# Gate products by one level of Strassen's algorithm, and a first layer without lead tiles

## The reference

```
h = _layer_norm(DN_ALPHA * h + u, ln2_g[i], ln2_b[i])
h = h + jax.nn.sigmoid(h @ ple_gate_w[i]) * (p[i] @ ple_w[i])
```

## Time and profile before

| | |
|---|---|
| three runs, median (lowest, highest) | 1969.9 us (1968.17, 1971.81) |
| profiled execution: its time | 1970.78 us |
| profiled execution: span, first to last instruction | 1969.0 us |
| mean granted TensorE clock | 0.998 |
| PE busy | 1945.6 us, 99% |
| DVE, POOL, ACT busy | 60%, 19%, 18% |
| chain that ended last | 90% PE, 4% issue, 2% DVE |

### The profile page before, as it was taken

The page is one execution under the profiler, slowest core; times in us unless marked ns, Lnnn a source line. Parts: engine busy times, 40 slices in busy tenths (PEclk is TensorE's granted clock), DMA queues, the critical chain, the costliest instruction groups (busy, mean ns, idle before and its releaser), DMA issues.

```text
span 1969.0 us, 33213 instructions
## 1 busy us (share of the span) xinstructions
PE 1945.6 (99%) x12520; PEld 1491.1 (76%) x12520; DVE 1181.2 (60%) x2268; ACT 351.0 (18%) x826; POOL 375.0 (19%) x485
## 2 busy tenths in 40 slices
PE   9999999999999999999999999999999999999998
PEld 7865994458769944599748869994799568769973
DVE  4343987533639875356754647666776636457674
ACT  2342000011420000300014522000200025321001
POOL 0000206310102064110130620004110303511012
PEclk9999999999999999999999999999999999999999
DMA  8422545534225454354443216444644443235443
GB/s 326 134 93 66 192 171 194 191 108 138 65 97 205 165 202 178 117 193 168 169 177 118 87 60 210 171 172 154 254 170 172 171 150 129 66 105 201 165 171 129
DMA packets 83806, 305.45 MB, mean 155 GB/s; under 512 B 9360, under 2 KB 10000, under 8 KB 83408
## 3 DMA queue, kind: packets, MB, share of 16 engines
q1 hardware_dynamic: 81360, 294.83, 42.6%
q0 software_dynamic: 2304, 8.65, 1.3%
HBM read 302.13 MB, written 1.05 MB: 154 GB/s over the span
## 4 chain that ended last, share of the span: by engine, by line
PE 90%; issue 4%; DVE 2%; ACT 1%; DVEq 0%; ACTq 0%; DMA 0%; POOL 0%; SPq 0%; POOLq 0%
PE psum L455 31%; PE psum L562 22%; PE psum L1022 13%; PE psum L2633 5%; PE psum L2033 4%; PE psum L467 3%; PE psum L337 3%; PE psum L248 2%; PE psum L326 2%; PE psum L1892 1%; PE psum L464 1%; PE psum L313 1%; PE psum L292 1%; PE psum L3019 1%; DVE x L873 0%
## 5 line engine op out<-in xcount | busy, mean ns | idle before, releaser
L455 PE MATMUL psum<-sq,space 128*128 128x128 f32 x2784 | 345.9, 275 | 1.6 <-DVE sq L659 1.6
L455 PEld LDWEIGHTS psum<-sq,space 128*128 128x128 f32 x2784 | 327.9, 192 | 2.2 <-issue 2.1
L754 POOL TENSOR_TENSOR cat<-space 128x128 f32<-128x128 f32 x76 | 57.9, 762 | 797.3 <-PE psum L562 550.6
L562 PE MATMUL psum<-space,cat 128*128 128x512 f32 x456 | 207.2, 592 | 0.0
L562 PEld LDWEIGHTS psum<-space,cat 128*128 128x128 f32 x456 | 86.4, 190 | 109.3 <-issue 109.3
L562 PE MATMUL psum<-ring,space 128*128 128x512 f32 x304 | 141.8, 592 | 0.0
L1022 PE MATMUL psum<-h,ring 128*128 128x256 f32 x544 | 124.5, 382 | 0.0
L455 PE MATMUL psum<-h,ring 128*128 128x128 f32 x928 | 122.6, 275 | 0.0
L455 PE MATMUL psum<-h,space 128*128 128x128 f32 x928 | 122.6, 275 | 0.0
L455 PE MATMUL psum<-sq,ring 128*128 128x128 f32 x928 | 120.9, 275 | 0.0
L439 DVE TENSOR_TENSOR space<-ring 128x512 f32<-128x512 f32 x76 | 59.4, 781 | 92.3 <-PE psum L562 92.3
(11 more groups left out here) (439 smaller groups left out, 3010.1 us busy)
## 6 DMA issues: line engine op xcount, KB each, us to landing
ring<-in_weights SPq DMA_DIRECT2D x551, 512.0 KB, 4.1
space<-in_rows POOLq DMA_DIRECT2D x8, 512.0 KB, 4.8
space<-in_gains POOLq DMA_DIRECT2D x6, 512.0 KB, 4.7
const<-in_consts SPq DMA_DIRECT2D x1, 1397.0 KB, 10.3
h<-in_x SPq DMA_DIRECT2D x4, 256.0 KB, 4.7
x<-in_x_tok SPq DMA_DIRECT2D x1, 1024.0 KB, 16.8
out<-x SPq DMA_DIRECT2D x2, 512.0 KB, 2.8
space<-in_params POOLq DMA_DIRECT2D x2, 509.5 KB, 4.8
```

What stands on the lines that cost most here:

```text
L455: last = pe.matmul(out, weights(i), tokens(i), start=(i == 0), stop=(i == 3), skip_group_check=True)
L562: return pe.matmul(k.psum[:, bank, :], lhs, rhs, start=(p == 0), stop=(p == fn.downs - 1), skip_group_check=True)
```

## The change

- `LEADS` becomes all zero: Ffn(2) opens with `first_jobs` and has 22 jobs in place of four leads and 18 jobs. POOL makes the weight sums of its job 0 when the layer-1 gate is summed; PE waits for three of the four summed quarters ahead of job 1.
- The gate product becomes one Strassen product over four pairs of row tiles (k, k + 4): parts 1, 2, 3, 6, 5, 7, 4, each four products of 128x512. DVE makes four token sums into `cat` and eight weight sums, POOL the other eight; part 3 waits for the token sums, part 6 for DVE's weight sums, part 7 for POOL's. DVE recombines the parts into four quarters; each goes through sigmoid, product with the embedding and sum.
- The embedding product goes column half by column half into the same banks, and ACT copies it to SBUF (`emb`), since the parts need banks 4 to 6.
- In layer 1 the first RMS norm of the second block uses half squares, so that the first half can be taken before the second is there.
- The order of the gate's units in memory goes pair by pair.

```diff
-LEADS, FIRST, TAIL, HELD = (0, 0, 4, 0, 0, 0), 4, 4, 4
+LEADS, FIRST, TAIL, HELD = (0, 0, 0, 0, 0, 0), 4, 4, 4
+PAIRS = KD // 2
+GATE_PARTS = 7
-FIRST_JOBS_AFTER = (border(0, 0, LN1), border(0, 1, LN1), border(1, 0, 1), border(1, 0, 2), border(1, 1, 1))
+FIRST_JOBS_AFTER = (border(0, 0, LN1), border(0, 1, LN1), border(0, 1, PLE), border(1, 0, 1), border(1, 0, 2), border(1, 1, 1))
...
-        pe_ffn(k, s, pe, w, Ffn(2 + 2 * l), g - 1, g, 5 if l else 4, k.h_tok, True, (k.y_half, 4 * l) if l else None)
+        pe_ffn(k, s, pe, w, Ffn(2 + 2 * l), g - 1, g, 5 if l else 4, k.h_tok, True, (k.y_half, 4 * l) if l else (k.gate_summed, 4 * LAYERS - 1))
...
+        else:
+            pool.wait_ge(k.gate_summed, 4 * LAYERS)
+            pool_first_sums(k, s, pool, Ffn(2))
...
@@ tail_tensor
+    pe.wait_ge(f.emb_copied, 4 * layer + 1)
+    for p in range(PAIRS):
+        last = part(1, p)
...
+    for p in range(PAIRS):
+        last = part(2, p)
+    last.then_inc(f.gate_parts, 1)
+    pe_normed(k, pe, ln2, 1)
+    pe.wait_ge(f.gate_tokens, layer + 1)
+    for p in range(PAIRS):
+        last = part(3, p)
+    last.then_inc(f.gate_parts, 1)
+    pe.wait_ge(f.emb_copied, 4 * layer + 3)
+    for p in range(PAIRS):
+        pe.wait_ge(f.gate_left, PAIRS * layer + p + 1)
+        last = part(6, p)
+    last.then_inc(f.gate_parts, 1)
+    for p in range(PAIRS):
+        last = part(5, p)
+    last.then_inc(f.gate_parts, 1)
+    for p in range(PAIRS):
+        pe.wait_ge(f.gate_right, PAIRS * layer + p + 1)
+        last = part(7, p)
+        if p < PAIRS - 1:
+            last.then_inc(k.freed, 2)
+    last.then_inc(f.gate_parts, 1)
+    for p in range(PAIRS):
+        if p == (3 if layer == LAYERS - 1 else 2):
+            pe_turn_h(k, pe, ple, 0, k.h_tok if layer == LAYERS - 1 else k.x_tok)
+        last = part(4, p)
...
@@ tail_scalar
+    squash(0, 0, 0)
     if layer == LAYERS - 1:
         act.wait_ge(s.params, 16)
+        act.wait_ge(f.x_half_new, 1)
+        act_half_square(k, s, act, 0, k.x_tok[:, 0, 0:512], 1.0, RMS_EPS)
+        squash(1, 0, 1)
+        act_root_table(k, act)
         act.wait_ge(s.x_new, 1)
+        act_root_of_sum(k, s, act, 0, k.x_tok[:, 0, 512:1024], 1.0).then_inc(s.x_std, 1)
+        squash(2, 1, 1)
+        act_first_turned(k, s, act, n, 0, "ffn1_pre_g")
+        squash(3, 1, 0)
+        act.wait_ge(f.x_half_new, 2)
+        act_half_square(k, s, act, 1, k.x_tok[:, 1, 512:1024], 1.0, RMS_EPS)
+        act_root_table(k, act)
         act.wait_ge(s.x_new, 2)
+        act_root_of_sum(k, s, act, 1, k.x_tok[:, 1, 0:512], 1.0).then_inc(s.x_std, 1)
+        act_first_turned(k, s, act, n, 1, "ffn1_pre_g")
         return
...
@@ tail_vector
+    dve.wait_ge(k.h_low, 2 * ln2 + 2)
+    dve.drain()
+    dve.tensor_tensor(x[:, 0, :, :], first[:, :, high], second[:, :, high], ALU.add)
+    dve.tensor_tensor(x[:, 2, :, :], first[:, :, low], first[:, :, high], ALU.subtract)
+    dve.drain()
+    dve.tensor_tensor(x[:, 1, :, :], x[:, 0, :, :], first[:, :, low], ALU.subtract)
+    dve.drain()
+    dve.tensor_tensor(x[:, 3, :, :], second[:, :, low], x[:, 1, :, :], ALU.subtract).then_inc(f.gate_tokens, 1)
+    for p in range(PAIRS):
+        b11, b12, _, _ = gate_unit_halves(k, dve, layer, p)
+        dve.tensor_tensor(f.sums[:, p, 0, :], b12, b11, ALU.subtract)
+    dve.drain()
+    for p in range(PAIRS):
+        _, _, _, b22 = gate_unit_halves(k, dve, layer, p)
+        dve.tensor_tensor(f.sums[:, p, 1, :], b22, f.sums[:, p, 0, :], ALU.subtract).then_inc(f.gate_left, 1)
...
+    dve.tensor_tensor(y(0, 0), k.copied, k.psum[:, 0, :], ALU.add).then_inc(k.gate_summed, 1)
...
+    gated(0, 0, 0)
+    added(0, 0).then_inc(f.x_half_new if last_layer else k.h_scaled, 1)
...
+    dve.tensor_tensor(y(1, 0), k.upper, k.psum[:, 2, :], ALU.subtract).then_inc(k.gate_summed, 1)
...
@@ tail_pool, behind the residual terms of LN2
+    for p in range(PAIRS):
+        _, b12, _, b22 = gate_unit_halves(k, pool, layer, p)
+        pool.tensor_tensor(f.sums[:, p, 2, :], b22, b12, ALU.subtract)
+    for p in range(PAIRS):
+        _, _, b21, _ = gate_unit_halves(k, pool, layer, p)
+        pool.wait_ge(f.gate_left, PAIRS * layer + p + 1)
+        pool.tensor_tensor(f.sums[:, p, 3, :], f.sums[:, p, 1, :], b21, ALU.subtract).then_inc(f.gate_right, 1)
```

More of the change, by code:

```diff
@@ L3014, in tail_tensor @@
     pe.wait_ge(k.parts_free, layer + 1)
[L3015 to L3018, removed]
+    rows = [pe_take(k, pe, w) for _ in range(2)]
+    for tt in range(2):
+        for b in range(2):
+            for c in range(2):
                 last = pe.matmul(k.psum[:, 4 + 2 * tt + b, :], f.embed[:, layer * 2 + c, half(tt)],
-                                 unit[:, b * 512:b * 512 + 512], start=(c == 0), stop=(c == 1), skip_group_check=True)
-                if tt + b == 0:
+                                 rows[c][:, b * 512:b * 512 + 512], start=(c == 0), stop=(c == 1),
+                                 skip_group_check=True)
+                if tt + b + c == 0:
@@ L3022, in tail_tensor @@
                     pe_hand_back(k, w, last)
-        w.owed += 1
+            last.then_inc(f.emb_ready, 1)
+    w.owed += 2
     pe_turn_h(k, pe, ln2, 1, k.h_tok)
     pe_normed(k, pe, ln2, 0)
[L3027 to L3032, removed]
+    units = [(pe_take(k, pe, w), pe_take(k, pe, w)) for _ in range(PAIRS)]
@@ new lines, in part @@
+    def part(name, p):
+        (a, c), sums, x = units[p], f.sums[:, p, :, :], f.gate_x
+        bank, lhs, rhs = {
+            1: (4, k.h[:, p, half(0)], a[:, 0:512]), 2: (0, k.h[:, PAIRS + p, half(0)], c[:, 0:512]),
+            3: (1, x[:, 3, p, :], c[:, 512:1024]), 4: (2, k.h[:, PAIRS + p, half(1)], sums[:, 3, :]),
+            5: (6, x[:, 0, p, :], sums[:, 0, :]), 6: (5, x[:, 1, p, :], sums[:, 1, :]),
+            7: (3, x[:, 2, p, :], sums[:, 2, :])}[name]
+        return pe.matmul(k.psum[:, bank, :], lhs, rhs, start=(p == 0), stop=(p == PAIRS - 1), skip_group_check=True)
@@ L3035, in tail_scalar, with embedding @@
+    last.then_inc(f.gate_parts, 1)
 def tail_scalar(k, f, s, act, w, layer):
+    def embedding(tt, b):
+        i = 2 * tt + b
+        act.wait_ge(f.emb_ready, 4 * layer + i + 1)
+        act.activation(f.emb[:, tt, b * 512:b * 512 + 512], k.psum[:, 4 + i, :], ACT.Copy).then_inc(f.emb_copied, 1)
     def norm(which, gain, bias):
@@ L3047, in norm @@
             last.then_inc(k.h_low, 1)
+            if which == LN2:
+                for b in range(2):
+                    embedding(tt, b)
     norm(LN1, "ln1_g", "ln1_b")
@@ L3145, in tail_vector @@
     norm(LN2, "ln2_g", "ln2_b")
[L3146 to L3151, removed]
-        dve.drain()
[L3153 to L3160, removed]
+    n, ln2 = border(0, layer, PLE), border(0, layer, LN2)
@@ new lines, in tail_vector @@
+    low, high, x = half(0), half(1), f.gate_x
+    first, second = k.h[:, 0:PAIRS, :], k.h[:, PAIRS:KD, :]
+    dve.wait_ge(k.h_low, 2 * ln2 + 2)
[6 more added lines that the diff above has]
+    dve.tensor_tensor(x[:, 3, :, :], second[:, :, low], x[:, 1, :, :], ALU.subtract).then_inc(f.gate_tokens, 1)
@@ new lines, in tail_vector @@
+    dve.drain()
+    dve.tensor_tensor(y(1, 1), k.upper, k.psum[:, 6, :], ALU.add).then_inc(k.gate_summed, 1)
+    if last_layer:
+        dve_rms_gained(k, s, dve, n, -1, 0, "ffn1_pre_g")
+    else:
+        turned_high(0)
+    gated(2, 1, 1)
+    dve.wait_ge(f.gate_parts, at + 7)
+    dve.tensor_tensor(y(1, 0), k.upper, k.psum[:, 2, :], ALU.subtract).then_inc(k.gate_summed, 1)
+    right = added(1, 1)
+    if last_layer:
+        right.then_inc(f.x_half_new, 1)
+    gated(3, 1, 0).then_inc(k.y_done, 1)
@@ new lines, in tail_vector, with gate_unit_halves @@
+    left = added(1, 0)
+    if last_layer:
+        left.then_inc(s.x_new, 1)
+        dve_rms_gained(k, s, dve, n, -1, 1, "ffn1_pre_g")
+    else:
+        left.then_inc(k.h_scaled, 2)
+        turned_high(1)
+def gate_unit_halves(k, eng, layer, p):
+    out = []
+    for j in range(2):
+        u = FFN_UNITS[layer] + 2 * FF1 + 2 + 2 * p + j
+        eng.wait_ge(k.filled[u % RING], 16 * (u // RING + 1))
+        out += [k.ring[:, u % RING, 0:512], k.ring[:, u % RING, 512:1024]]
+    return out
@@ L3428, in first_tail_units @@
     units = ffn_units([v["mlp_w1"][l]], v["mlp_w2"][l], LEADS[l])
-    gate, ple = list(v["ple_gate_w"][l].reshape(KD, P, UNIT)), list(v["ple_w"][l].reshape(2, P, UNIT))
-    return units + ple + gate
+    gate, ple = v["ple_gate_w"][l].reshape(KD, P, UNIT), list(v["ple_w"][l].reshape(2, P, UNIT))
+    return units + ple + [gate[p + half] for p in range(PAIRS) for half in (0, PAIRS)]
 def first_params(v):
```

68 lines of the change are left out of this document (55 added, 13 removed).

## The result

The changed kernel takes 1974.7 us (median of 20 runs, 1971.4 to 1976.4) against 1970.2 for the one before (20 runs, 1968.0 to 1973.5): ratio 1.0020, 95% interval 1.0014 to 1.0027. The forecast was 1972.7 in 1965 to 1977. The interval leaves out 1, so the change makes the kernel slower by 0.14 to 0.27%. The profiled execution has a span of 1974.4 us and a time of 1976.2.

What follows compares the result with a forecast made beforehand. TensorE, busy 1945.6 of 1969.0 us, was taken as the bound; 10.4 us of work and 0.4 of old wait removed against new waits gave +2.8 us, or 1972.7 us on the median's scale, range 1965 to 1977.

Steps and rivals of the forecast that it cites:

- Work removed, 10.4 us: TensorE work saved: 3.43 us in each of two gates and 3.57 us from replacing Ffn(2)'s lead tiles.
- The engines take turns: VectorE and GpSimd wait for each other's whole SBUF-to-SBUF instruction; turns of 0.55 us for VectorE, 0.96 or 1.12 for GpSimd's sums.
- Rival 1: The engines hardly hold each other up: no waits in the gates, -8.4 us, 1961.5; chance 0.17.
- Rival 2: GpSimd keeps VectorE out for its full 1.27 us in every sum: +5.4 us, 1975.3, slower; chance 0.20.
- Each gate 1.0 us later: In both layers' gates, 4.4 us of new TensorE waits stand against 3.43 us of work removed.
- Opening of Ffn(2), 0.95 and 3.75 us of waits: Second block's start: TensorE waits 0.95 us at the second token half's transposes and 3.75 us in job 0's blocks.
- No cost behind job 4, none from the copies, the ring or POOL's memset: Ffn(2)'s later jobs, the embedding copies, the weight units and GpSimd's wait behind the memset were to add no time.
- rival 3: Ffn(2) without leads falls behind later on VectorE's added sums: 3 to 4 us more than forecast, 1976; chance 0.08.
- The sum, +2.8 us: Whole kernel: work -10.4, old wait -0.4, gates +4.4 twice, opening +0.95 and +3.75, restarts +0.1.
- the 0.1 us allowed for restarts: Over all waits on the path: each restarts TensorE a few hundredths of a us later than counted, +0.1 in all.

Runs made afterwards that it cites:

- e3: The changed kernel with GpSimd's gate weight sums cut from 512 to 8 columns, the rest not computed; layer 0's gate takes 24.91 us.
- e4: The changed kernel with all sixteen weight sums of a gate on VectorE and none on GpSimd; ratio 0.9985 to the kernel before.
- e6: The changed kernel with twelve of sixteen gate weight sums on VectorE, GpSimd making part 4's four behind them; ratio 0.9983 to the kernel before.
- e2: The kernel before's gates kept, only the four lead tiles of Ffn(2) replaced by four more Strassen jobs; ratio 1.0018 to the kernel before.
- e7: The changed kernel with e6's gate sums and the weight sums of Ffn(2)'s job 0 on VectorE; ratio 0.9965 to the kernel before.

## Why the prediction was right, and where its numbers were off

- *Work removed, 10.4 us.* Right. Where no sum of GpSimd's is in the way (e3), layer 0's gate is 3.43 us shorter to the hundredth.
- *The engines take turns.* Right, with 1.12 us for GpSimd's turn and 0.55 for VectorE's. I forecast the token sums' ends, counted from the gate's start, at 5.06, 6.71 and 8.36 us; they came at 5.11, 6.78 and 8.45. Rival 1 (no hold, 1961.5) fell with the 2.84 us; e3, which makes its condition nearly true in the gates, shows its gates' price. Rival 2 (a full 1.27 us per turn, 1.82 in all) isn't what the trace shows: 1.67. The Trainium skill ("SBUF — State Buffer", section "SBUF: two separate sides") has an exclusive lock, taken for the whole instruction, between a VectorE instruction with two SBUF inputs and one of GpSimd's that reads SBUF. The trace agrees on the blocking (2.84 us for 0.69), and a sum with one input in PSUM isn't held (0.67 us); but the turn is shorter than the instruction's shown duration, 1.12 of 1.27 us. Two sums of the rivals are off, with no effect on the reading: rival 1's terms give -8.15 us, not -8.4, and rival 2's +5.4 leaves out the 0.5 us that the opening already costs in the forecast.
- *Each gate 1.0 us later.* Mis-sized: 1.63 and 1.70. The idle times add up to 4.05 us, less than the 4.4 forecast, but idle time is not all that a wait costs. By the pitch of 0.429 us the first instruction of part 3 was due at 404.66 + 16 x 0.429 = 411.52 and came at 413.25: 1.73 us for a wait shown as 1.56, since the record of the matmul before runs 0.16 us over its pitch. Counted so, part 3 is delayed by 1.73 us (1.6 forecast), part 6 by 1.95 (1.8) and by 0.47 + 0.81 (1.0), and 0.11 are lost behind it: 5.07 us, of which 3.43 are earned back. The shortfall, some 0.6 us a gate and 1.3 us in both, lies for the most part in VectorE's chain. Its last weight sum for part 6 was drawn 17.26 us behind the gate's start (420.3) and ended at 17.78 (422.44), 0.52 late. 0.34 of that is one term: the forecast gave GpSimd's sums of the form "space<-space,ring" a turn of 0.96 us, from the 1.09 us of the earlier trace rows, and counted 1.50 us for a pair; the last three of VectorE's sums came 1.67 apart, so the turn was 1.12. The trace of the kernel before had this price: in the first block, where the gates lie, GpSimd's sum of the same form takes 1.27 us in both layers, and 1.09 only in the second block. What makes the two differ isn't shown.

```profile
199.28 1.27 POOL L740 TENSOR_TENSOR space<-space,ring 128x512 f32<-128x512 f32 x1 [0.51 <-issue]
```

Another 0.09 is the token sums' late end, and the rest of the shortfall is small delays along the chain and PE's restarts, for which the forecast had +0.1 in all. With 1.12 us for every sum of GpSimd's the forecast would have been 1973.2, by its own count.
- *Opening of Ffn(2), 0.95 and 3.75 us of waits.* Right. Counted from the last gate's end I had the second half's transposes at 6.3 us, job 0's four blocks at 10.6, 12.2, 13.7 and 15.4, and job 4 at 30.6. In e4, which has the same opening code and a clock of 1.00 in it, they came at 6.14, 10.49, 12.16, 13.66, 15.34 and 30.59; in the changed kernel the transposes and the first two blocks at 6.28, 10.63 and 12.31, then under the low clock the fourth block at 15.65 and job 4 at 31.03.
- *No cost behind job 4, none from the copies, the ring or POOL's memset; rival 3.* Right as far as the rows tell: behind job 4 the only growth is 1.48 us, with 3.4 us of low clock in it, and nothing waits at the transposes behind layer 0's gate.
- *The sum, +2.8 us, forecast 1972.7.* The touched stretches gave +4.3, the medians +4.5. 1.3 us of the difference are the gates and 0.4 the clock in the opening; both errors went the same way, and the 0.1 us allowed for restarts and the rounding of the sum take 0.2 off. The forecast called this no change, since 3.9 us could hardly be told from none. With 20 runs of each kernel it can: the direction that it named, slower, is what the interval shows.

The spread between executions goes with the clock, which I had left out of the account. Sorted by their mean granted clock, the 55 runs of the kernel before on the experiments' chips average 1968.1 us at 1.000 (9 runs), 1969.4 at 0.999 (19), 1970.8 at 0.998 (16), 1972.4 at 0.997 (7) and 1974.1 at 0.996 (4): what I took for noise is ordered by it. The changed kernel's 20 runs, measured at another time, average 1971.9 (2 runs), 1973.0, 1973.5, 1974.9 and 1976.1 at the same clocks: 3.8 us more at 1.000, 2.0 more at 0.996, and 2.7 on the average of its runs. Its mean clock is lower, 0.9975 against 0.9984. Whether the change itself brings on the lower clock is open: in the five openings with these waits it fell in two profiled executions (the changed kernel, e6) and not in three (e2, e3, e4); in the five openings without them it never fell. A low stretch that lies in a wait costs less than one that lies in work (0.4 us against 1.7), so the 2.7 is rather too low for the change's waits; the 3.8 us of its touched stretches at full clock (4.27 less 0.44) is the other estimate, and it is what the two runs at 1.000 show.

## What to carry to other kernels

Moving these sums from VectorE to GpSimd added no capacity while both read and wrote SBUF: a VectorE sum (0.55 us of turn) and a GpSimd sum (1.12) together take 1.67 us, and two sums of VectorE's 1.22 (0.61 each). Before splitting such work, list what VectorE has to deliver at that time; here the same sums all on VectorE were faster (e4), and GpSimd was free help only where VectorE waited or read from PSUM (0.67 us for a sum beside GpSimd's). Look up a price in the block where the work will lie: the same form cost 1.27 us in one and 1.09 in the other. A saving in matmuls is worth its pitch only if the operand sums in front of it fit in the time that the products before them give, and each wait cost PE 0.17 to 0.26 us more than the idle time shown.

## What the hardware showed that I had not expected

- The granted clock falls to 0.50 for 3.4 or 6.8 us at a time, from never (e4, e7) to three times, 13.7 us in all (the changed kernel), before the last 20 us of a profiled execution. Some places come back: 140 to 150 us in eight of the ten profiled executions, 830 to 850 and 1120 to 1140 us in the changed kernel and e6; 520 to 530 us has it only in the kernel before. It falls also where PE is busy throughout: in the changed kernel PE is busy for 10.00 of 10.00 us from 1120 to 1130 and from 1130 to 1140, where the clock falls. Executions of the kernel before differ by some 6 us with it (1968.1 to 1974.1 on the average of equal clocks).
- A matmul's idle time is under-told by 0.16 us: instructions of 128x512 last 0.592 us in the record and follow each other every 0.429.
- VectorE holds GpSimd up as well, even in short sums. In e3 the first of GpSimd's four 8-column sums takes 0.65 us beside VectorE's second token sum. The second, for which no sum of VectorE's stands in front, ends at 408.30, some 0.2 us behind the first, so by estimate a short sum's fixed cost is at most that. VectorE's sums beside them take their solo 0.69 us.

```profile
407.49 0.65 POOL L3347 TENSOR_TENSOR space<-ring 128x8 f32<-128x8 f32 x1
407.49 0.81 POOL L3347 TENSOR_TENSOR space<-ring 128x8 f32<-128x8 f32 x2
```
